# Up projections of three feed-forward layers: the order of three ScalarE operations within one unit

## The chip, the cores and the metric

One core of a Trainium2 chip runs the whole program. The time is the device time of one execution in microseconds (us). Of the kernel before there are three timed executions: 1224.78, 1225.55 and 1227.5 us, median 1225.55 us. One further execution was recorded by the hardware profiler; all rows below come from it.

## The reference

The input is 256 tokens of 1024 channels in float32. One layer of a first kind is followed by two layers of a second kind. Each layer projects the tokens, mixes them in three branches (attention, a recurrence or a pooling, a gated convolution or a second attention), adds the result to the stream, normalizes, and ends with a feed-forward part. The feed-forward part is what matters here:

```
u  = causal_conv3(h @ w_up)        # 1024 -> 2 * 2816 channels, 3 taps over the tokens
a, b = split(u, 2)
x  = x + act(a) * b @ w_down       # act: gelu in the first layer, silu in the two others
```

## The kernel before, in words

Channels stand on the 128 partitions and the 256 tokens on the free axis. All weights stream from HBM once, in 400 *units* of 128 output channels by up to 1024 input channels (512 KB, or 448 KB for seven blocks). To keep float32 accuracy TensorE works with split operands: a weight tile `raw` becomes a high part `whi` (a rounded copy, ScalarE, line 735) and a low part `wlo = raw - whi` (VectorE, line 1393), and each 128x128 block takes three matmuls: `whi` with the high activations (line 1067), `whi` with the low ones (1068), `wlo` with the high ones (1069). A whole unit is 24 matmuls.

`raw`, `whi` and `wlo` are rings of three tiles. Unit n waits on TensorE for `wlo` of unit n (`split_lo`). ScalarE may write `whi` of unit n+3 when unit n is done on TensorE (`unit_done`) and the load has landed (`arrived`). SyncE issues the load of unit n+3 when VectorE has written `wlo` of unit n. The result banks in PSUM are also a ring of three.

Each engine has its own instruction stream, written out in a fixed order, and works through it in order. There is no planner in this part. The up projection of a layer has 44 units: even ones give a tile of `a` (the gate), odd ones the matching tile of `b`. The first six and the last eight units are written out, those between run in a hardware loop of six. I call the units of one up projection 0 to 43, and those of the down projection behind it 44, 45, 46 and so on. The three stages are `up1` (first layer), `up20` and `up21`.

The work on one up unit, in the order of the engines' programs:

- ScalarE (`ffn`, lines 991 to 1020): the high part of the unit two ahead; then it waits for the unit; the eviction (lines 1007, 1009: it reads the bank, scales by the last tap and writes `ugate` or `uval`). After an odd unit it applies the activation to `ugate` (line 1014), after an even unit it waits for GpSimd's product of the pair before and copies it to `fhi` (`high`, line 995).
- VectorE (`up`, lines 1731 to 1743): the low part of the unit two ahead (line 1393), then the two other taps, which read the bank (lines 1738, 1741). The second one frees the bank.
- GpSimd (`ffn`, lines 621 to 641): for each pair the product `fprod = ugate * uval` (line 636), which waits for both taps and for the activation; and then the low part `flo` of the pair before (line 625). For the last pair the low part stands alone behind the loop.

The first activation of each up projection is preceded by a load of ScalarE's function table. The down projection (24 units of 8, 7 and 7 blocks) needs all 22 tiles of `fhi` and `flo`: its third unit, number 46, waits for `flo` of the last tile (line 1332). Between an up projection and what precedes it stands a normalization. Units 0 and 1 are computed interleaved, block by block, as the normalized tiles come in; in `up20` and `up21` GpSimd is meanwhile still writing the residual stream (line 702).

Of the kernel before, what the change touches and what calls it, by code (L numbers as in the profile page):

```python
# [16 lines left out]
UPT = 2 * FT  # L17
# [34 lines left out]
def unit_table():  # L52

    units, start = [], {}

    def phase(name, array, tiles, parts):
        start[name] = len(units)
        for t in range(tiles):
            at = 0
            for n in parts:  # L60
                units.append((array, t, at, n))
                at += n

    start["win1"] = 0
    units += [("w_win1", t, 0, 8) for t in PLAN1]
    phase("merge1", "w_merge1", KT, (8, 8))
    phase("wout1", "w_out1", KT, (8,))
    phase("up1", "w_up1", UPT, (8,))
    phase("down1", "w_down1", KT, DOWN_PARTS)
    for l in range(LAYERS2):  # L70
        start[f"win2{l}"] = len(units)
        units += [(f"w_win2{l}" if kind == "in" else f"w_merge2{l}", t, 0, 8) for kind, t in PLAN2]
        phase(f"wout2{l}", f"w_out2{l}", KT, (8,))
        phase(f"up2{l}", f"w_up2{l}", UPT, (8,))
        phase(f"down2{l}", f"w_down2{l}", KT, DOWN_PARTS)
    return units, start


UNITS, START = unit_table()
# [120 lines left out]
def build(nc, args, out):  # L200
# [3 lines left out]
    with ctx:  # L204
# [137 lines left out]
        def wait(eng, s, base, it=0, per=0):  # L342

            if isinstance(it, int):
                if base + it * per > 0:
                    eng.wait_ge(s, base + it * per)
            else:
                eng.wait_ge(s, it * per + base)

        def repeat(eng, name, count, per, body, peel_first=False):  # L350

            rounds = count // per
            lo, hi = (1 if peel_first else 0), rounds - 1
            n0 = START[name]
            for i in range(lo * per):
                body(n0 + i, i, 0)
            if hi > lo:
                with eng.Fori(lo, hi) as it:  # L360
                    for i in range(per):
                        body(n0 + i, i, it)
            for i in range(hi * per, count):
                body(n0 + i, i, 0)
# [34 lines left out]
        def tile(ten, t, it=0, per=0):  # L399

            return ten[:, t:t + 1, :] if isinstance(it, int) else ten[:, bass.ds(it * per + t, 1), :]

        def tap(cols, width, k, i, it):

            a = COLS[cols] + width * i + k
            return vec[:, a:a + 1] if isinstance(it, int) else vec[:, bass.ds(it * (6 * width) + a, 1)]
# [35 lines left out]
        def bank_of(r):  # L442
            return unit_bank[r % 3]
# [283 lines left out]
        def _(act):  # L727
            def hi_part(n, it=0, per=0):
                if n >= len(UNITS):
                    return  # L730
                blocks = UNITS[n][3]

                wait(act, arrived[n % RING], 16 * (n // RING + 1), it, 16 * per // RING)
                wait(act, unit_done, n - RING + 1, it, per)
                act.activation(whi[:, n % RING, 0:blocks * P], raw[:, n % RING, 0:blocks * P], ACT.Copy).then_inc(split_hi, 1)  # L735
# [255 lines left out]
            def ffn(f, name, cols, silu):  # L991
                def high(t, it=0):

                    wait(act, product, FT * f + t + 1, it, 3)
                    act.activation(tile(fhi, t, it, 3), tile(fprod, t % 3), ACT.Copy).then_inc(f_hi, 1)  # L995

                def body(n, i, it):
                    if i or not isinstance(it, int):
                        hi_part(n + 2, it, 6)
                    p, r = FT * f + i // 2, (i // 2) % 3  # L1000
                    wait(act, unit_done, n + 1, it, 6)

                    wait(act, product, p - 2, it, 3)

                    ps, dst = bank_of(RESULT[name] + i)[:, 0:S], (ugate, uval)[i % 2][:, r, :]
                    if silu:
                        act.activation(dst, ps, ACT.Copy, scale=tap(cols, 3, 2, i, it)).then_inc(conv_start, 1)
                    else:
                        act.activation(dst, ps, ACT.Identity, scale=tap(cols, 4, 2, i, it), bias=tap(cols, 4, 3, i, it)) \
                            .then_inc(conv_start, 1)  # L1010
                    if i % 2:

                        wait(act, conv_done, KT + 2 * p + 1, it, 6)
                        act.activation(ugate[:, r, :], ugate[:, r, :], ACT.Silu if silu else ACT.Gelu_apprx_tanh).then_inc(gelued, 1)
                    elif i or not isinstance(it, int):
                        high(i // 2 - 1, it)

                repeat(act, name, UPT, 6, body, peel_first=True)
                hi_part(START[name] + UPT + 2)
                high(FT - 1)  # L1020

            wout(START["wout1"], "ffn")
# [1 line left out]
            hi_part(START["up1"] + 2)  # L1024
            norm_hi("ffn", dev)
            ffn(0, "up1", "ffn_1", False)
            down("down1", "final")
            norm_root("final", RMS_EPS)
# [3 lines left out]
            for l in range(LAYERS2):  # L1032
                first = START[f"win2{l}"]
                waiting = None
                for p, (kind, t) in enumerate(PLAN2):
                    n = first + p
                    if kind == "in":
                        act.wait_ge(unit_done, n + 1)
                        ps = bank_of(RESULT[f"win2{l}"] + p)[:, 0:S]
                        dst = pads[:, 0, t - 6, 16:16 + S] if t in (6, 7) else u2[:, t, :]  # L1040
                        if t < 14:
                            act.activation(dst, ps, ACT.Copy).then_inc(copied, 1)
                        else:
                            act.activation(dst, ps, ACT.Tanh, scale=0.5).then_inc(copied, 1)
                    steps(n, first + MIX2)
                    if waiting is not None:
                        merged_hi(KT * (1 + l), waiting)
                    waiting = t if kind == "merge" else None
                merged_hi(KT * (1 + l), KT - 1)
                wout(START[f"wout2{l}"], f"ln1{l}", 1)  # L1050
                norm_root(f"ln1{l}", LN_EPS)
                hi_part(START[f"up2{l}"] + 2)
                norm_shift(f"ln1{l}", False)
                ffn(1 + l, f"up2{l}", f"ffn_2{l}", True)
                down(f"down2{l}", f"ln2{l}")
                norm_root(f"ln2{l}", LN_EPS)
                if l < LAYERS2 - 1:
                    hi_part(START[f"win2{l + 1}"] + 2)
                norm_shift(f"ln2{l}", l == LAYERS2 - 1)
# [860 lines left out]
```

## Time and profile before

| what | value |
|---|---|
| median of three executions | 1225.55 us |
| profiled execution, its own time | 1226.56 us |
| span from the first to the last instruction in it | 1224.7 us |
| mean granted TensorE clock | 0.993 |
| TensorE matmul busy | 1206.6 us (99%) |
| TensorE weight load busy | 1183.0 us (97%) |
| VectorE busy | 846.1 us (69%) |
| ScalarE busy | 707.7 us (58%) |
| GpSimd busy | 406.6 us (33%) |
| mean of DMA over the span | 174 GB/s |

The busy time of TensorE counts matmuls that overlap in its pipeline: one is recorded with some 0.28 us although the next starts much sooner. So a lost moment is best read from the starts of two neighbouring matmuls, not from the busy share. Idle time that the profile shows in brackets is counted from the modelled end of the matmul before.

### The profile page before, as it was taken

The numbers are of one execution on the slowest core, as the hardware profiler recorded it, in microseconds if no ns is written. First come the engines' busy times: TensorE is split into PE (matmuls) and PEld (weight loads), VectorE is DVE, ScalarE is ACT, GpSimd is POOL, SyncE is SP. The second block draws the span as 40 slices with busy tenths as digits, with TensorE's granted clock in tenths as the row PEclk, the third lists the DMA queues.
The fourth block names the chain that finished last, engine by engine and source line by source line (L and its number), as shares of the span: only waits on it lengthen the run. The fifth ranks groups of instructions, "written<-read, shape, count | busy, mean of one in ns | idle before, by whom it ended". The sixth has DMA issues, their size and how long they took to land. (4 is left out here: it accounts for less than half of the span.)

```text
span 1224.7 us, 27264 instructions
## 1 busy us (share of the span) xinstructions
PE 1206.6 (99%) x10242; PEld 1183.0 (97%) x10242; DVE 846.1 (69%) x1458; ACT 707.7 (58%) x1228; POOL 406.6 (33%) x376
## 2 busy tenths in 40 slices
PE   8999999999999999999999999999999999999997
PEld 8999999999999999999999999999999999999997
DVE  6868666677777755766677777656766677777655
ACT  5667676445766654566455666644566555666642
POOL 3007304123334302200338343314500348344313
PEclk9999999999999999999999999999999999999998
DMA  7555455664666665555653666664555654666662
GB/s 254 183 168 156 134 153 166 197 182 154 194 187 201 183 191 162 164 164 155 190 185 116 183 190 187 195 190 147 171 157 156 190 187 121 178 199 186 196 189 85
DMA packets 60288, 212.70 MB, mean 174 GB/s; under 512 B 6688, under 2 KB 7968, under 8 KB 60064
## 3 DMA queue, kind: packets, MB, share of 16 engines
q1 hardware_dynamic: 60192, 211.39, 56.6%
q8 instruction: 65, 1.06, 0.4%
q14 instruction: 31, 0.25, 0.1%
HBM read 210.31 MB, written 1.05 MB: 173 GB/s over the span
## 5 line engine op out<-in xcount | busy, mean ns | idle before, releaser
L1393 DVE TENSOR_TENSOR wlo<-raw,whi 128x1024 fp32r<-128x1024 f32 (+1 forms) x400 | 488.5, 1222 | 289.4 <-ACT whi L735 287.5
L1067 PE MATMUL bank<-shifted,whi 128*128 128x256 f32 x2296 | 638.9, 278 | 1.5 <-POOL shifted L669 1.1
L1068 PE MATMUL bank<-shifted,whi 128*128 128x256 f32 x2296 | 636.3, 277 | 0.0
L1069 PE MATMUL bank<-shifted,wlo 128*128 128x256 f32 x2296 | 636.0, 277 | 0.0
L735 ACT ACTIVATE whi<-raw 128x1024 fp32r<-128x1024 f32 (+1 forms) x400 | 415.6, 1040 | 148.0 <-PE bank L1069 134.4
L1067 PEld LDWEIGHTS bank<-shifted,whi 128*128 128x128 f32 x2296 | 431.7, 188 | 3.1 <-POOL shifted L669 1.3
L1069 PEld LDWEIGHTS bank<-shifted,wlo 128*128 128x128 f32 x2296 | 431.7, 188 | 0.0
L1068 PEld LDWEIGHTS bank<-shifted,whi 128*128 128x128 f32 x2296 | 431.1, 188 | 0.0
L636 POOL TENSOR_TENSOR fprod<-ugate,uval 128x256 f32<-128x256 f32 x66 | 99.4, 1506 | 210.1 <-DVE uval L1741 204.5
L1067 PE MATMUL bank<-fhi,whi 128*128 128x256 f32 x528 | 146.8, 278 | 0.0
L1069 PE MATMUL bank<-fhi,wlo 128*128 128x256 f32 x528 | 146.5, 277 | 0.0
L1068 PE MATMUL bank<-flo,whi 128*128 128x256 f32 x528 | 146.5, 277 | 0.0
L650 POOL TENSOR_TENSOR u<-u,tmp 128x256 f32<-128x256 f32 x48 | 53.7, 1119 | 234.1 <-DVE tmp L1696 232.0
L1067 PE MATMUL bank<-aligned,whi 128*128 128x256 f32 x334 | 105.2, 315 | 4.2 <-DVE wlo L1393 2.2
L1069 PEld LDWEIGHTS bank<-fhi,wlo 128*128 128x128 f32 x528 | 99.7, 189 | 0.0
L1067 PEld LDWEIGHTS bank<-fhi,whi 128*128 128x128 f32 x528 | 99.1, 188 | 0.1
L1068 PEld LDWEIGHTS bank<-flo,whi 128*128 128x128 f32 x528 | 99.1, 188 | 0.0
L1069 PE MATMUL bank<-aligned,wlo 128*128 128x256 f32 x334 | 93.3, 279 | 0.0
L1068 PE MATMUL bank<-aligned,whi 128*128 128x256 f32 x334 | 92.4, 277 | 0.0
L995 ACT ACTIVATE fhi<-fprod 128x256 f32 (+1 forms) x66 | 27.6, 418 | 100.4 <-POOL fprod L636 100.4
L1067 PEld LDWEIGHTS bank<-aligned,whi 128*128 128x128 f32 x334 | 62.8, 188 | 14.4 <-issue 9.0
L1068 PEld LDWEIGHTS bank<-aligned,whi 128*128 128x128 f32 x334 | 62.9, 188 | 0.7
(212 smaller groups left out, 1283.3 us busy)
## 6 DMA issues: line engine op xcount, KB each, us to landing
raw<-in_w_win SPq DMA_DIRECT2D x140, 512.0 KB, 3.6
raw<-in_w_up SPq DMA_DIRECT2D x132, 512.0 KB, 3.6
raw<-in_w_down SPq DMA_DIRECT2D x48, 448.0 KB, 3.8
raw<-in_w_merge SPq DMA_DIRECT2D x32, 512.0 KB, 4.1
raw<-in_w_out SPq DMA_DIRECT2D x24, 512.0 KB, 3.8
raw<-in_w_down SPq DMA_DIRECT2D x24, 512.0 KB, 3.6
x<-in_x SPq DMA_DIRECT2D x4, 256.0 KB, 3.9
rgw<-in_rg_w SPq DMA_DIRECT2D x1, 1024.0 KB, 10.2
```

Source lines behind the costliest of these rows:

```text
L636: pool.tensor_tensor(tile(fprod, t % 3), tile(ugate, t % 3), tile(uval, t % 3), ALU.mult).then_inc(product, 1)
L650: ins = pool.tensor_tensor(m, m, branch_part(base, t, branch), ALU.add)
L735: act.activation(whi[:, n % RING, 0:blocks * P], raw[:, n % RING, 0:blocks * P], ACT.Copy).then_inc(split_hi, 1)
L995: act.activation(tile(fhi, t, it, 3), tile(fprod, t % 3), ACT.Copy).then_inc(f_hi, 1)
L1067: pe.matmul(ps, whi[:, slot, w], hi, start=first, stop=False)
L1068: pe.matmul(ps, whi[:, slot, w], lo, start=False, stop=False)
L1069: return pe.matmul(ps, wlo[:, slot, w], hi, start=False, stop=last)
L1393: dve.tensor_tensor(wlo[:, n % RING, w], raw[:, n % RING, w], whi[:, n % RING, w].bitcast(f32), ALU.subtract) \
```

## The change

The high part of a unit is now issued by the body of the unit three before it, behind the eviction and in front of the activation (odd units) or of the wait for the product and its copy (even units). Before, it was issued at the head of the body of the unit two before it. Between two evictions the order was therefore eviction, activation or copy, high part; now it is eviction, high part, activation or copy. The set of instructions, their tiles and their semaphores stay the same; the high part that stood behind the loop is now issued by the last body.

```diff
                 def body(n, i, it):
-                    if i or not isinstance(it, int):
-                        hi_part(n + 2, it, 6)
                     p, r = FT * f + i // 2, (i // 2) % 3
                     wait(act, unit_done, n + 1, it, 6)
...
                         act.activation(dst, ps, ACT.Identity, scale=tap(cols, 4, 2, i, it), bias=tap(cols, 4, 3, i, it)) \
                             .then_inc(conv_start, 1)
+                    hi_part(n + 3, it, 6)
                     if i % 2:
 
                         wait(act, conv_done, KT + 2 * p + 1, it, 6)
...
                 repeat(act, name, UPT, 6, body, peel_first=True)
-                hi_part(START[name] + UPT + 2)
                 high(FT - 1)
```

## Rows read from the trace of the kernel before

**Rows 1.** Windows: stretch, its length, busy us and instructions by engine, PEclk, DMA share, GB/s.
```profile
311.00:418.00 107.00, 107.00 (x940) 107.00 (x939) 81.26 (x119) 70.68 (x118) 44.68 (x40) 1.00 0.64 194
...
849.60:853.00 3.40, 3.31 (x14) 2.92 (x13) 2.95 (x8) 2.18 (x4) 3.40 (x5) 0.50 0.00 0
```
**Rows 2.** Waits of TensorE: who waited for whom, us in total, times, longest us.
```profile
PE bank L1067 <- DVE wlo L1393: 2.2, 2, 1.1
```
**Rows 3.** Timeline, TensorE early in up20: start us, us, engine, line, tiles.
```profile
670.93 0.28 PE L1069 MATMUL bank<-shifted,wlo 128*128 128x256 f32 x1
...
671.54 0.28 PE L1068 MATMUL bank<-aligned,whi 128*128 128x256 f32 x1
...
674.13 0.28 PE L1069 MATMUL bank<-shifted,wlo 128*128 128x256 f32 x1
...
675.70 0.28 PE L1068 MATMUL bank<-aligned,whi 128*128 128x256 f32 x1
```
**Rows 4.** Timeline, VectorE's low parts of units 4 and 5 in up20.
```profile
669.93 1.33 DVE L1393 TENSOR_TENSOR wlo<-raw,whi 128x1024 fp32r<-128x1024 f32 x1 [0.90 <-ACT whi L735]
...
674.19 1.23 DVE L1393 TENSOR_TENSOR wlo<-raw,whi 128x1024 fp32r<-128x1024 f32 x1 [2.02 <-ACT whi L735]
```
**Rows 5.** Timeline, ScalarE early in up20, from the eviction of unit 1.
```profile
666.75 0.47 ACT L1007 ACTIVATE uval<-bank,vec 128x256 f32<-128x256 f32 x1
667.23 1.28 ACT L1014 ACT_TABLE_LOAD   x1
668.53 0.42 ACT L1014 ACTIVATE ugate<-ugate 128x256 f32<-128x256 f32 x1
668.85 1.05 ACT L735 ACTIVATE whi<-raw 128x1024 fp32r<-128x1024 f32 x1
669.80 0.45 ACT L1007 ACTIVATE ugate<-bank,vec 128x256 f32<-128x256 f32 x1
672.79 0.42 ACT L995 ACTIVATE fhi<-fprod 128x256 fp32r<-128x256 f32 x1 [2.54 <-POOL fprod L636]
673.12 1.04 ACT L735 ACTIVATE whi<-raw 128x1024 fp32r<-128x1024 f32 x1
```
**Rows 6.** Timeline, TensorE at the third unit of the down projection behind up20.
```profile
788.39 0.28 PE L1069 MATMUL bank<-fhi,wlo 128*128 128x256 f32 x1
...
789.18 0.28 PE L1068 MATMUL bank<-aligned,whi 128*128 128x256 f32 x1
```
**Rows 7.** Timeline, end of up20: the last eviction on ScalarE.
```profile
783.73 0.45 ACT L1007 ACTIVATE uval<-bank,vec 128x256 f32<-128x256 f32 x1
```
**Rows 8.** Timeline, end of up20: VectorE.
```profile
783.85 1.09 DVE L1393 TENSOR_TENSOR wlo<-raw,whi 128x896 fp32r<-128x896 f32 x1 [1.01 <-ACT whi L735]
...
785.38 0.48 DVE L1741 SCALAR_TENSOR_TENSOR uval<-bank,vec,uval 128x254 f32<-128x254 f32 x1
```
**Rows 9.** Timeline, end of up20: GpSimd.
```profile
785.93 1.52 POOL L636 TENSOR_TENSOR fprod<-ugate,uval 128x256 f32<-128x256 f32 x1 [2.71 <-DVE uval L1741]
787.41 1.43 POOL L625 TENSOR_TENSOR flo<-fprod,fhi 128x256 fp32r<-128x256 f32 x2
```
**Rows 10.** Timeline, TensorE at unit 4 of up1 and at unit 46 behind it.
```profile
308.49 0.28 PE L1069 MATMUL bank<-shifted,wlo 128*128 128x256 f32 x1
...
309.06 0.28 PE L1068 MATMUL bank<-aligned,whi 128*128 128x256 f32 x1
...
423.54 0.28 PE L1069 MATMUL bank<-fhi,wlo 128*128 128x256 f32 x1
...
424.09 0.28 PE L1068 MATMUL bank<-aligned,whi 128*128 128x256 f32 x1
```
**Rows 11.** Timeline, TensorE at unit 5 of up21.
```profile
1040.98 0.28 PE L1069 MATMUL bank<-shifted,wlo 128*128 128x256 f32 x1
...
1042.61 0.28 PE L1068 MATMUL bank<-aligned,whi 128*128 128x256 f32 x1
```
**Rows 12.** DMA issues: tiles, queue, count, KB each, median us from issue to landing.
```profile
raw<-in_w_up SPq DMA_DIRECT2D x132, 512.0 KB, 3.6
```

## The prediction

> **What bounds the kernel now.** I read the windows first. In the quiet middle of up1 TensorE starts 940 matmuls in 107.00 us at a granted clock of 1.00, its level of 2.4 GHz: one every 0.114 us, without a hole [rows 1]. A unit of 24 takes 2.73 us, and no reordering on ScalarE shortens that. What such a change can give back is the sum of the places where TensorE waited for something behind ScalarE's queue. So I read TensorE's waits next: two long ones, 2.2 us in all, are for `wlo` at the head of a unit [rows 2]. Then I went along the timeline of TensorE and looked in the three up projections for two matmul starts further apart than 0.114 us. Three places stand out in up20; I measure each from the last matmul of one unit to the second of the next, less two steps (0.23 us), which also catches the slow restart of the first matmul:
>
> - unit 4: 670.93 to 671.54, lost 0.38 us [rows 3];
> - unit 5: 674.13 to 675.70, lost 1.34 us [rows 3];
> - unit 46, the third of the down projection: 788.39 to 789.18, lost 0.56 us [rows 6].
>
> up21 has the same three: its unit 5 loses 1.40 us [rows 11], and the two others repeat up20's within 0.04 us (0.38 and 0.60). up1 has two small ones, 0.34 us at unit 4 and 0.32 us at unit 46 [rows 10]. The sum over the three layers is 0.66 + 2.28 + 2.38 = 5.3 us, 0.43% of the time. That is the ceiling for the direct gain.
>
> **Unit 4 and unit 5: why they wait.** The low part of unit 4 ends at 671.26, that of unit 5 at 675.42, each just ahead of the matmul that starts late; both times VectorE had been idle until the high part was there [rows 4]. On ScalarE the first activation brings a table load of 1.28 us. Behind the eviction of unit 1 at 666.75 come table load, activation, and only at 668.85 the high part of unit 4; then the eviction of unit 2, a wait of 2.54 us for the first product of GpSimd, its copy at 672.79, and only at 673.12 the high part of unit 5 [rows 5]. Both high parts needed nothing of what stood ahead of them.
>
> **The same stretch in the new order**, with durations of these rows and the pipelining that they show (the next activation starts about 0.1 us before the recorded end of the one before):
>
> - ScalarE: high part of unit 4 from 667.2 to 668.25, table load to 669.55, activation to 669.95, eviction of unit 2 from 669.9 to 670.35 (0.1 later than now), high part of unit 5 from 670.3 to 671.35, copy of the product still at 672.8 (GpSimd sets it), eviction of unit 3 from 673.1, high part of unit 6 to 674.6.
> - Load of unit 5: it goes out when the low part of unit 2 is written, so before TensorE starts unit 2, two units ahead of unit 4, at about 671.04 - 5.46 = 665.6; with a median landing of 3.6 us [rows 12] it is there by 669.2, ahead of 670.3.
> - VectorE keeps its order (low part of unit n+2, taps of unit n, 0.5 us each). The low part of unit 4 now follows the taps of unit 1 and ends at about 670.3; TensorE wants it at 671.04. The low part of unit 5 ends at 672.6; wanted at 673.8. The low part of unit 6 follows the taps of unit 3 and ends at 675.9; wanted at 676.5.
>
> Unit 5 then has 1.2 us to spare. What is late next is unit 6, with 0.6 us; its term hangs on GpSimd's first product. I count both holes as gone: 0.38 + 1.34 in up20, 0.38 + 1.40 in up21, and 0.34 in up1, where the same table load stands: 3.84 us. Bounds: 2.5 us, if half an us reappears at unit 6 in the two late layers and up1 keeps its hole, and 3.84 us, since the holes can't give more.
>
> **Inside the loops** the edit costs and gives nothing: there is no hole now. The cover is the ring of three: after an eviction a bank is wanted two units (5.5 us) later, and the activation and the copy are pushed back by one high part, 1.05 us. The copy at even units waited for the product anyway, so the high part fills that idle time. A high part asked for earlier must find its load landed. Its issue hangs on the low part three units before, which moves forward as well: the landing comes some 1.5 us ahead of the request at the median of 3.6 us, and a late one holds ScalarE, not TensorE.
>
> **Unit 46** waits for `flo` of the last tile. The chain before it: last eviction at 783.73, just behind the end of unit 43 on TensorE (the next unit starts 44 steps before 788.39, at 783.4), so it can't move; VectorE is at that moment busy with the low part of unit 45 until 784.94, and only then the two taps, to 785.86 [rows 7, 8]; product 785.93 to 787.45, two low parts to 788.84 [rows 9]. In the new order the high part of unit 45 stands ahead of the copy, its low part is over before the last eviction, and the taps end at 785.25. But the last activation now stands behind the high part of unit 46: 784.2 to 785.15, activation to 785.5. So the product starts at 785.5 instead of 785.93. The activation takes the place of the taps as what ends last: 0.45 us gained of 0.6. I take 0.47 us in up20 and 0.5 in up21. In up1 evictions are 0.57 us long and the low part is started no later than here, so I take half its hole, 0.15. Sum 1.1 us. Bounds: from -0.6 us (three times 0.2, if the activation ends later than the taps do now) to 1.5 us, the whole holes.
>
> A rule of the skill bears on the product. The row shows it at 1.52 us here, and it overlaps the low part of unit 46 on VectorE [rows 9]. The Trainium skill, "SBUF — State Buffer", section "SBUF: two separate sides", says that GpSimd and a two-input VectorE operation take a shared port pair as an exclusive lock, so that the second one waits for the whole first. By that rule the product ends 0.6 us behind the low part of unit 46 whenever it starts inside it; the end would then move by how much that low part moves, again about 0.45 us, so the sum stays as it is.
>
> **Sum.** 3.84 + 1.1 = 4.9 us. The profiled execution would go from 1226.56 us to 1221.7 (span 1219.8). It is 1.0 us above the median of the runs, so for the median 1225.55 - 4.9 = 1220.7 us.
>
> **The rivals.**
>
> *The hole moves to unit 6.* For it: GpSimd writes the residual stream until just before the first product, and ScalarE waits for it (2.54 us, [rows 5]) ahead of the eviction of unit 3, on which the low part of unit 6 now hangs. Against it: 0.6 us of room. Price: with a product 1.3 us later 0.7 us come back in each of two layers. Gain 3.5 us, 1222.1 us.
>
> *The table load first empties ScalarE's pipeline.* The load would then wait for the end of the high part ahead of it and hold what follows by as much again, one high part (1.05 us). The eviction of unit 2 slips to 671.0, the low part of unit 5 to 673.7, and that of unit 6 to 677.0, so about 0.6 us come back per layer: gain 3.1 us, 1222.5 us. Against it: the rows show the load 0.01 us behind the end of an eviction and the activation 0.02 us behind the load [rows 5]. The Trainium skill, "ScalarE: Activation LUTs", section "What ACT_TABLE_LOAD costs", gives 1283 ns for the load, which the trace confirms with 1.28 us, and about 1380 ns of drain on top, which no row here shows. By its figure I would estimate some 0.3 us more per layer to come back.
>
> *Given back behind the up projections.* The down projections and normalizations start earlier, but their own chains (loads that land just in time, the norm's chain across four engines) do not. For it: ring and DMA work at 194 GB/s all the way [rows 1]. Against it: the loads hang on the same low parts, which come earlier. If half is lost, 1223.2 us; if all, 1225.5 us. I put the case at 1224.3.
>
> *Slower: the clock.* In a normalization TensorE idles, and the granted clock fell to 0.50 (1.2 GHz) for 3.4 us at 849.6 [rows 1], there mostly over filler matmuls. The change moves the five normalizations behind up1 in time. Where such a dip covers real products it costs half of it, 1.7 us. From three new dips (5.1 us) the gain is gone; with five it is 8.5 - 4.9 = 3.6 us slower, 1229.2 us. For it: the fall is seen in the profile; against it: it fell on filler, and nothing in the change lengthens the idle time.
>
> **How the numbers follow.** Chances: forecast 0.72, hole at unit 6 0.12, emptied pipeline 0.05, given back 0.07, clock 0.04. The predicted time is the first one's, 1220.7 us. Its bounds by the terms are 1225.55 - 5.3 = 1220.2 and 1225.55 - 1.9 = 1223.7. The three runs before lie up to 2 us above their median and 0.8 below it, so another median of few runs may lie about an us off: 1218.9 to 1223.6 us as the range, which takes in the first two rivals. A difference of 0.2% (2.45 us) is about what a measurement of this kernel can tell from no change; it lies at 1223.1. Faster: the first three cases with a little left out for scatter, 0.85; within 0.2%: 0.11, mainly gain given back; slower: 0.04.
>
> **What would show it.** Right: no start distance over 0.2 us at units 4 and 5 of up20 and up21; table load behind a high part; high part of unit 5 some 3 us ahead of the copy of the first product; the last product waiting for the activation and no longer for the taps. Wrong: a hole at unit 6 of up20, a wait of ScalarE for `raw` inside the loops that reaches TensorE, a hole of 0.3 us or more at unit 46, or a granted clock below 1.00 over real products.

## The result, and the profile after

The changed kernel takes 1218.08 us (median of four, 1217.63 to 1218.27); the kernel before 1225.82 us (median of four). The ratio is 0.9934, 95% interval 0.9923 to 0.9946: 7.7 us faster. The prediction was 1220.7 us with a range from 1218.9. The direction was right; the gain was half as large again as forecast and the time lies 0.8 us below the range. The profiled executions are further apart, 1226.56 and 1217.63 us, spans 1224.7 and 1215.8 us.

By the page of the changed kernel no engine's total moved by over 7 us, and ScalarE does the same work, 707.5 us against 707.7:

```profile
span 1215.8 us, 27264 instructions
## 1 busy us (share of the span) xinstructions
PE 1199.6 (99%) x10242; PEld 1177.9 (97%) x10242; DVE 852.5 (70%) x1458; ACT 707.5 (58%) x1228; POOL 404.3 (33%) x376
```

In the list of TensorE's waits the line for `wlo` [rows 2] is gone, and so are the waits for `flo`. The largest of what is left stand at the normalizations:

```profile
PE bank L1122 <- POOL acc L663: 3.9, 5, 2.4
PE bank L1065 <- POOL shifted L669: 1.1, 1, 1.1
```

Early in up20, ScalarE after the change (answers to [rows 5]; lines of this file behind 998 count two less, those from 1009 to 1017 one less):

```profile
663.63 0.47 ACT L1005 ACTIVATE uval<-bank,vec 128x256 f32<-128x256 f32 x1
663.99 1.06 ACT L735 ACTIVATE whi<-raw 128x1024 fp32r<-128x1024 f32 x1
665.07 1.28 ACT L1013 ACT_TABLE_LOAD   x1
666.36 0.42 ACT L1013 ACTIVATE ugate<-ugate 128x256 f32<-128x256 f32 x1
666.69 0.46 ACT L1005 ACTIVATE ugate<-bank,vec 128x256 f32<-128x256 f32 x1
667.04 1.05 ACT L735 ACTIVATE whi<-raw 128x1024 fp32r<-128x1024 f32 x1
670.17 0.42 ACT L995 ACTIVATE fhi<-fprod 128x256 fp32r<-128x256 f32 x1 [2.08 <-POOL fprod L636]
```

The high part of unit 4 now stands ahead of the table load, that of unit 5 3.1 us ahead of the copy of the product. TensorE in the same stretch, at the heads of units 4 and 5 (answers to [rows 3]):

```profile
668.12 0.28 PE L1067 MATMUL bank<-shifted,wlo 128*128 128x256 f32 x1
668.24 0.28 PE L1065 MATMUL bank<-aligned,whi 128*128 128x256 f32 x1
668.36 0.28 PE L1066 MATMUL bank<-aligned,whi 128*128 128x256 f32 x1
...
670.95 0.28 PE L1067 MATMUL bank<-shifted,wlo 128*128 128x256 f32 x1
671.07 0.28 PE L1065 MATMUL bank<-aligned,whi 128*128 128x256 f32 x1
671.18 0.28 PE L1066 MATMUL bank<-aligned,whi 128*128 128x256 f32 x1
```

The distance from the last matmul of a unit to the second of the next is 0.23 to 0.24 us at both heads, where it was 0.61 and 1.57: the holes are closed. The end of up20 after the change, ScalarE, VectorE and GpSimd (answers to [rows 7 to 9]):

```profile
778.14 0.47 ACT L1005 ACTIVATE uval<-bank,vec 128x256 f32<-128x256 f32 x1 [1.12 <-PE bank L1067]
778.51 0.95 ACT L735 ACTIVATE whi<-raw 128x896 fp32r<-128x896 f32 x1
779.36 0.41 ACT L1013 ACTIVATE ugate<-ugate 128x256 f32<-128x256 f32 x1
```
```profile
776.83 1.08 DVE L1391 TENSOR_TENSOR wlo<-raw,whi 128x896 fp32r<-128x896 f32 x1
...
779.17 0.48 DVE L1739 SCALAR_TENSOR_TENSOR uval<-bank,vec,uval 128x254 f32<-128x254 f32 x1
779.57 1.09 DVE L1391 TENSOR_TENSOR wlo<-raw,whi 128x896 fp32r<-128x896 f32 x1
```
```profile
779.89 1.36 POOL L636 TENSOR_TENSOR fprod<-ugate,uval 128x256 f32<-128x256 f32 x1 [3.25 <-DVE uval L1739]
781.21 1.44 POOL L625 TENSOR_TENSOR flo<-fprod,fhi 128x256 fp32r<-128x256 f32 x2
```

From the last eviction to the start of the last product it is 1.75 us; before it was 2.20, so 0.45 us less, as forecast. The product starts behind the activation (ends at 779.77) and no longer behind the taps (779.65), also as forecast; the row names VectorE as the releaser, but the activation's semaphore comes 0.11 us behind that of the taps. To the end of `flo` it is 4.51 us against 5.11.

Where the rest came from shows only when the times of the semaphore events are laid out by stage. For each stage this table has the time from the end of the last unit of the stage before to the end of its own last unit, before and after, the difference, and how many units were *slow*: the median distance of their matmul starts is over 0.1155 us.

```
stage        before    after    diff   slow units before / after
win1         226.20   225.76   -0.44   19 / 19
up1          126.77   126.25   -0.51    2 /  0
down1         62.72    60.56   -2.15   18 /  0
up20         132.19   129.83   -2.36    7 /  4
down20        61.80    61.00   -0.79    1 /  0
up21         131.60   129.66   -1.95    3 /  2
down21        61.84    61.00   -0.84    1 /  0
all others   421.62   421.75   +0.13   13 / 14
```

The biggest surprise is down1: 2.15 us in a stage whose code did not change. TensorE's step there, in windows of 37 us, first the kernel before, then the changed one:

```profile
438.00:475.00 37.00, 37.00 (x316) 37.00 (x315) 18.30 (x20) 16.37 (x20) 5.83 (x4) 1.00 0.66 196
```
```profile
438.00:475.00 37.00, 37.00 (x329) 37.00 (x329) 19.31 (x21) 16.67 (x22) 5.83 (x4) 1.00 0.70 203
```

316 matmuls against 329, at a granted clock of 1.00 in both: a mean step of 0.117 us against 0.1125, with no wait shown anywhere. By single starts within a unit TensorE has two steps, 0.118 and 0.1133 us; every unit of down1 from number 50 on runs at the longer one before, and none after. Where it begins, VectorE's low part of unit 50 and TensorE at the head of that unit, in the kernel before:

```profile
433.16 1.23 DVE L1393 TENSOR_TENSOR wlo<-raw,whi 128x1024 fp32r<-128x1024 f32 x1 [2.07 <-ACT whi L735]
```
```profile
434.45 0.28 PE L1069 MATMUL bank<-fhi,wlo 128*128 128x256 f32 x1
434.57 0.34 PE L1067 MATMUL bank<-fhi,whi 128*128 128x256 f32 x1
434.75 0.28 PE L1068 MATMUL bank<-flo,whi 128*128 128x256 f32 x1
434.87 0.28 PE L1069 MATMUL bank<-fhi,wlo 128*128 128x256 f32 x1
```

The low part is written at 434.39, the last matmul of unit 49 starts at 434.45; the second start of unit 50 comes 0.18 us behind its first, and from there on all distances are 0.118 us.

### The profile page after: what moved, and what is told of

It reads as the page before. It is cut to its first block, busy times and chain, and to the rows that moved or that the text cites. A ratio compares the mean times of both kernels' runs of the same rounds, so it can differ in the third digit from the quotient of the medians.

```text
span 1215.8 us, 27264 instructions
## 1 busy us (share of the span) xinstructions
PE 1199.6 (99%) x10242; PEld 1177.9 (97%) x10242; DVE 852.5 (70%) x1458; ACT 707.5 (58%) x1228; POOL 404.3 (33%) x376
## 4 chain that ended last, share of the span: by engine, by line
PE 89%; issue 4%; DVE 3%; POOL 3%; ACT 1%; DMA 0%; POOLq 0%; DVEq 0%; ACTq 0%
PE bank L1065 28%; PE bank L1067 27%; PE bank L1066 27%; POOL acc L663 2%; PE bank L1206 1%; PE bank L1237 1%; PE bank L1122 1%; PE bank L1081 1%; DVE wlo L1391 1%; PE bank L1217 1%; POOL acc L659 1%; PE bank L1261 1%; ACT whi L735 0%; POOL u L650 0%; PE bank L1193 0%
## 5 line engine op out<-in xcount | busy, mean ns | idle before, releaser
L1067 PEld LDWEIGHTS bank<-aligned,wlo 128*128 128x128 f32 x334 | 62.6, 187 | 0.0
```

The lines of the kernel that those rows point to most:

```text
L1067: return pe.matmul(ps, wlo[:, slot, w], hi, start=False, stop=last)
```

## The experiments

A margin below is the time from the writing of a unit's low part to the moment when TensorE wants it, at the last matmul start of the unit before. I call a short irregular step at the head of a unit a stumble. Each kernel is compared with the kernel before on its own chip: 1225.59 us in the first group, 1226.1 in the second, 1225.88 in the last. Microseconds of gain are differences of medians; the ratio with its interval, given beside them, puts those of the edits to the kernel before lower, by 0.3 to 0.9 us, and by 1.3 us in b_odd.

**b_sines**, the kernel before with one edit in down1, where unit 50 had a margin of 0.06 us:

```diff
-                    if name == "down1" and i == 3 and isinstance(it, int):
+                    if name == "down1" and i == 4 and isinstance(it, int):
                         step_prepare_sines()
                         load_sqrt()
```

> The kernel before, with one edit in the down projection of the first layer: the two sines and the table loads around them stand one body later, so that the high part of unit 50 goes ahead of them. Theory A (near miss): in the kernel before, the low part of unit 50 is written only 0.06 us before TensorE wants it, TensorE falls there into a step of 0.118 us per matmul instead of 0.113 and keeps it for the 18 units to the end of the stage, 1.8 us. With the high part earlier by over 2 us the step stays at 0.113: 1.8 us faster than before, near 1224.0 us. Theory B: the longer step belongs to the stage itself (its loop, its tiles) or is an accident of one execution: no change, within 0.5 us of before.

Measured: 1224.67 us (11 runs), ratio 0.9995, 95% interval 0.9986 to 1.0004. In the profile unit 50 has a margin of 2.21 us, no unit of down1 is slow, and down1 takes 60.74 us instead of 62.72:

```profile
438.00:475.00 37.00, 37.00 (x329) 37.00 (x328) 19.15 (x20) 16.10 (x20) 5.84 (x4) 1.00 0.70 205
```

So the trace says theory A, and the time does not decide: the medians differ by 0.9 us, half of what A gives, and the interval runs from 1.7 us faster to 0.5 us slower. Either the edit costs elsewhere, or the kernel before does not have the long step in all executions. That led to the last group.

**a_late**, the changed kernel with a tiny activation ahead of the high part of unit 50:

```diff
                         step_prepare_sines()
                         load_sqrt()
+                        act.activation(small[:, 88:89], small[:, 92:93], ACT.Copy)
```

> The changed kernel with one tiny activation (one column, about 0.2 us) added on ScalarE in the down projection of the first layer, ahead of the high part of unit 50. The low part of unit 50 there has 0.13 us to spare. Theory A: it becomes some 0.07 us late, TensorE loses 0.1 to 0.2 us at the head of that unit and then 0.1 us in each of 18 units: 1.9 us slower than the changed kernel, near 1220.0 us. Theory B: the delay itself and nothing more, 0.1 to 0.2 us: near 1218.2 us.

Measured: 1217.61 us, ratio 0.9945 (0.9931 to 0.9958). A miss for A as written. The activation cost only 0.11 us, as neighbours overlap; the margin fell to 0.04 us, unit 50 lost 0.09 us, and the short step stayed in the profiled execution. But the five times are 1217.17, 1217.61, 1217.61, 1219.04 and 1220.11, where the changed kernel's four lie within 0.64 us.

**a_sines**, the changed kernel with the edit of b_sines.

> The changed kernel with the sines one body later, as in the other run. Theory A: the margin of unit 50 was 0.13 us and just enough; nothing to win, within 0.3 us of the changed kernel (1218.1). Theory B: the same. If the changed kernel still lost in some executions to the longer step, its spread would shrink and its median fall.

Measured: 1217.57 us (1217.45 to 1217.93), margin 2.29 us, down1 60.56 us as in the changed kernel. Nothing to win there, as both theories said. It is not a faster version that I could tell from the changed kernel (0.9938 against 0.9934, with intervals 0.0025 wide).

**b_loop, b_start, b_end**: the kernel before with the high part moved only in some bodies. The edit is the same in all, with `early` as `not isinstance(it, int)` (loops), `isinstance(it, int) and i < 6` (start) and `isinstance(it, int) and i >= 36` (end):

```diff
-                    if i or not isinstance(it, int):
-                        hi_part(n + 2, it, 6)
...
+                    if early:
+                        hi_part(n + 3, it, 6)
                     if i % 2:
...
+                    if not early:
+                        hi_part(n + 3, it, 6)
...
-                hi_part(START[name] + UPT + 2)
```

Behind the activation or the copy of one body is the same place in ScalarE's order as the head of the next, so where `early` is false the order is that of the kernel before.

> The new order only in the hardware loops (units 6 to 35 of the three up projections); the first six and last eight units in the old one. Theory A: the low parts of the odd units, which in the kernel before run down to margins of 0.1 us and below, get 2 us; the three stumbles in the loops (units 21 and 33 of up20, unit 31 of up21) go: 0.33 + 0.33 + 0.2 = 0.9 us faster, near 1224.9 us; the holes at units 4, 5 and 46 stay; down1 keeps its longer step unless unit 50's margin moves by chance. Theory B, that of my prediction (nothing to gain inside the loops): no change.

Measured: 1222.59 us, ratio 0.9981 (0.9972 to 0.9990): 3 us faster, not 0.9 and not nothing. In the profile up20 lost 1.01 us and up21 0.24, mostly the stumbles; and down20 and down21 lost 0.79 and 0.84, since the margin at the heads of units 46 and 47 depends on what the loop hands over. Down1 lost the long step, but its unit 46 starts 0.67 us later.

> The new order only in the first six units of each up projection, the old one in the loops and in the last eight. By the direct count of the starts the holes at units 4 and 5 go, 3.8 us; what the near misses in the loops do is open: the margins at the loop's start are larger, so that they may never run down to zero, which would give another 0.9 us. Near 1221.5 us, 1220.9 at best. Rival: the stall moves to unit 6, only 2.5 us gained.

Measured: 1221.03 us, ratio 0.9964 (0.9950 to 0.9977), 5.1 us faster. up1, up20 and up21 lost 0.51, 2.27 and 2.21 us: the holes, and of the stumbles those of up21. With a better start the margins of up21's loop stay at 0.11 us and more. Those of up20 still ran down to -0.04 us by unit 33: its units 21, 27 and 33 took 2.83, 2.88 and 2.91 us where 2.74 is due, though none turned slow. Unit 6 did not become a hole (margin 0.11 us, 0.02 us lost). Down1 took 63.70 us: 0.8 us longer at unit 46, and the long step for that unit and all that followed. The reason for the 0.8 us, at the end of up1 of b_start, VectorE and GpSimd, and TensorE at unit 46 (VectorE's lines count two more here than in the kernel before):

```profile
419.91 1.61 DVE L1395 TENSOR_TENSOR wlo<-raw,whi 128x896 fp32r<-128x896 f32 x1
422.04 1.23 DVE L1395 TENSOR_TENSOR wlo<-raw,whi 128x1024 fp32r<-128x1024 f32 x1 [0.51 <-ACT whi L735]
```
```profile
419.84 0.74 POOL L636 TENSOR_TENSOR fprod<-ugate,uval 128x256 f32<-128x256 f32 x1 [2.71 <-DVE uval L1743]
420.54 3.31 POOL L625 TENSOR_TENSOR flo<-fprod,fhi 128x256 fp32r<-128x256 f32 x2
```
```profile
423.99 0.35 PE L1069 MATMUL bank<-aligned,whi 128*128 128x256 f32 x1 [0.77 <-POOL flo L625]
```

The product starts 0.07 us ahead of the low part and takes 0.74 us, and the low part takes 1.61 instead of 1.09. In the changed kernel and in the one before the low part was first and the product took 1.36 and 1.52 us [rows 9]. The first `flo` operation then runs beside the rest of this low part and takes 1.59 us, the second beside the next low part, which starts 0.05 us ahead of it, and takes 1.76: 3.31 us for the two instead of 1.43. That agrees with the Trainium skill, "SBUF — State Buffer", section "Who interferes with whom": the order of issue decides which of the two is held.

> The new order only in the last eight units of each up projection. The holes at unit 46 and the restarts at unit 47 go: 0.3 + 0.8 + 0.8 = 1.9 us. In the first layer TensorE then comes to unit 50 0.3 us earlier and ScalarE about as much: margin as in the changed kernel or as in the one before; if the former, the longer step goes as well and it is 3.7 us in all. Between 1222.1 and 1223.9 us.

Measured: 1222.91 us, ratio 0.9978 (0.9968 to 0.9987), 3.2 us faster, inside what I gave. Down1 60.56, down20 61.00, down21 61.00 us, to the hundredth what they are in the changed kernel. So for the down stages the last eight units are enough. The three parts give 3.0, 5.1 and 3.2 us, more than the 7.7 of the whole, since two of them can each remove the same stumbles, the same holes at unit 46 (b_loop and b_end both have down20 and down21 at 61.00 us) and the same long step.

**b_odd and b_even**: the same edit with `early = i % 2 == 1` (ahead of the activation) and `early = i % 2 == 0` (ahead of the copy).

> The high part ahead of the activation at odd units only; at even units it stays behind the copy of the product. The hole at unit 4 goes (1.1 us over three layers), that at unit 5 stays, since its high part still stands behind the first product. Even units at the end gain little. If the activation is the culprit of half: 1.1 to 2.0 us faster, near 1224 us.

Measured: 1224.99 us, ratio 1.0002 (0.9993 to 1.0012): no gain that can be told by the ratio, though the median is 1.1 us lower; a miss. In up20 the hole at unit 4 is gone, and units 2 to 5 together still take 12.71 us against 12.84: unit 5 starts when its low part is there, and that has not moved. ScalarE shows why: the high part of unit 5 starts behind the copy, and the copy waits for GpSimd, whose time the edit doesn't move.

```profile
668.22 0.46 ACT L1005 ACTIVATE ugate<-bank,vec 128x256 f32<-128x256 f32 x1
671.16 0.42 ACT L995 ACTIVATE fhi<-fprod 128x256 fp32r<-128x256 f32 x1 [2.49 <-POOL fprod L636]
671.49 1.04 ACT L735 ACTIVATE whi<-raw 128x1024 fp32r<-128x1024 f32 x1
```

> The high part ahead of the wait for the product and its copy at even units only; at odd units it stays behind the activation. The hole at unit 5 goes (2.8 us), that at unit 4 stays; unit 46 gains (the low part of unit 45 is early, and the last activation stands ahead of the high part of unit 46, so the last product starts earlier than in the changed kernel): all of 1.9 us. The odd units' margins, which run down in the loops, hang on this high part: 0.9 us more. Some 5 us faster, near 1220.5 us; the odd part alone then does little.

Measured: 1220.58 us, ratio 0.9962 (0.9950 to 0.9975), 5.5 us faster, as forecast. up20 lost 2.43 and up21 1.74 us with no slow unit in up20, and down20 and down21 are at 61.00 us. The even units carry the change.

**again1, again2, again3**: the kernel before, unchanged, for more profiles; and **a_late2**, the changed kernel with an activation of 256 columns in place of the tiny one:

```diff
+                        act.activation(probT[:, 0, 0:S], const[:, 0:S], ACT.Copy)
```

> The kernel before once more, unchanged, for another profile. What is open is whether the longer step of down1 (18 units at 0.118 us per matmul, 1.8 us in all) is the same in every execution. Theory A (a near miss with a coin toss): the margin at unit 50 is the same 0.06 us each time, and the step stays short in some executions and turns long in others; an execution with the short step takes down1 in some 60.9 us, one with the long step 62.7. Theory B (fixed by the program): down1 takes 62.7 us in each.

> The same as again1, a second profile. Theory A: the two may differ by 1.8 us in down1. Theory B: they don't.

> The same as again1, a third profile. Theory A and B as there.

Measured, with the first profile of the kernel before:

```
             before   again1   again2   again3
time        1226.56  1225.72  1224.42  1224.87
margin u.50    0.06     0.05     0.04     0.04
unit 50        2.89     2.89     2.82     2.82
down1         62.72    62.58    60.93    60.93
slow units       18       18        0        0
```

The same program, the same margin, two outcomes 1.7 us apart: theory A. (b_odd, whose unit 50 has a margin of 0.05 us, is a third profile without the long step in down1.) TensorE in again2, in the same window as above:

```profile
438.00:475.00 37.00, 37.00 (x329) 37.00 (x328) 19.07 (x20) 16.62 (x21) 5.83 (x4) 1.00 0.68 207
```

The stumbles of the loops come and go as well: in again2 unit 21 of up20 takes 2.77 us, in the first profile 2.98 us with a slow unit behind it. So does the hole at unit 4 of up20: in again1 and again3 unit 4 takes 2.78 us, and units 2 and 3 are 0.2 us longer together instead.

> The changed kernel with an activation of 256 columns (0.3 us net) ahead of the high part of unit 50 in down1: its low part is some 0.2 us late in every execution. Theory A: each execution pays the hole and its restart, 0.2 to 0.4 us, and a share of them 1.8 us more for the longer step; the times fall into two groups, near 1218.0 and near 1220 us. Theory B (the delay alone counts): one group near 1218.0 us with the narrow spread of the changed kernel.

Measured: 1217.86, 1218.76, 1219.34, 1219.43 and 1220.94 us, median 1219.34. Margin -0.18 us in the profile, unit 50 takes 3.12 instead of 2.72 us, all 18 units are slow, down1 62.62 us instead of 60.56:

```profile
438.00:475.00 37.00, 37.00 (x316) 37.00 (x316) 19.16 (x20) 15.43 (x20) 5.81 (x4) 1.00 0.66 199
```

So 0.3 us of ScalarE time at this place cost 2.06 us in that execution. The times spread over 3 us; two clean groups they are not. The ratio, 0.9946 (0.9932 to 0.9961), does not part it from the changed kernel, but four of the five times lie above all nine of the changed kernel and a_sines. Theory B, a narrow group near 1218.0 us, falls.

**Margins over all profiles.** The 14 profiles of these kernels hold 2303 units of the up and down projections, from the sixth of each on, that follow a unit at the short step. Of the 2178 with a margin over 0.115 us none took 0.02 us more than is due and none turned slow (by the mean of its last eight distances). Of the 125 with less, 28 turned slow. So in these stages the longer step set in only where a low part came late or less than 0.12 us early; in which of those cases it does is not explained.

## Why the prediction was wrong

The forecast was 4.9 us of gain and the medians show 7.7. Of the 2.8 us between them the term for unit 46 has some 0.9, the loops, put at nothing, 0.9, and down1, which stood in no term, 0.9. With them the ceiling of 5.3 us falls as well: it counted only holes of over 0.3 us. The range, too, left little room there: 1.3 us below the bound of 1220.2 us.

**Unit 4 and unit 5.** Right, in mechanism and size. I had 3.84 us for the three layers. From the durations of units 2 to 6 in up20 and the same in up1 and up21 it is 3.8 us: 0.38, 1.57 and 1.81. up20 stayed below its term since units 2 and 3 there run 0.09 and 0.20 us longer after (low part of unit 3 late by 0.09 us). That is scatter and no cost of the change: a_late2 and a_sines have these units at 2.74 us, and again1 and again3 have them longer in the kernel before. So the close hit is in part luck of the two profiles. b_odd shows that the two holes are one chain, and that the hole at unit 4 alone was worth nothing where another stood behind it; my sum added them, which holds only because both went.

**Unit 46.** The chain came as written, but the term was mis-sized: I took 1.1 us of gain at the three ends, the traces give 0.33 + 0.79 + 0.84 = 1.96. Two things were left out. The head of unit 47 had lost 0.2 us in each late layer, which I had not looked at (2.94 and 2.95 us where 2.72 is due; 2.85 to 2.87 us in again1 to again3). And the product got shorter, 1.36 instead of 1.52 us, since VectorE's low part, which holds it, had moved forward by 0.6 us and not by the 0.45 that I set. The bound of 1.5 us was too low for the first reason.

**"Inside the loops the edit costs and gives nothing: there is no hole now."** This is the step that failed. I looked for idle time and took a row of up1 [rows 1] for all three loops. In up20 and up21 the low part of every second unit arrived mostly 0.1 to 0.4 us before it was wanted, but 0.05 and 0.04 us too late at units 21 and 33 of up20 and only 0.08 us early at unit 31 of up21: these are the three stumbles, 0.86 us in the profile. After the change the margin in the loops is some 2 us. b_loop measures the step by itself: 3 us by the medians, where I had nothing. Some 1.2 us of that show inside up20 and up21, the rest in the down stages, to which the loops hand on their margins.

**Down1** stood in no term. The stumble at unit 50 at a margin of 0.06 us put TensorE on the longer step for 18 units: 1.83 us of the profile's 8.9. In half of the four profiles of the kernel before it did so, thus, as an estimate from four draws, some 0.9 us of the mean. That also accounts for the profile's larger difference (8.9 against 7.7 of the medians), with 0.44 us in win1, a stage that the change doesn't touch and that varies by as much between profiles of one kernel.

The sum with what was measured: 3.8 + 2.0 + 0.9 + 1.8 + 0.4 = 8.9 us for the profiled pair, against 3.8 + 1.1 forecast.

**The rivals.** No hole opened at unit 6 of up20 (margin 0.54 us, 0.6 forecast). In up21 the margin there is only 0.11 us, and units 6 and 7 run at the longer step, 0.17 us in all; a_sines and a_late2 show the same. The room that the forecast gave this rival was not there in up21. No emptying of the pipeline: the table load starts 0.02 us behind the end of the high part, and the activation 0.01 us behind the load; the drain that the Trainium skill adds in "ScalarE: Activation LUTs", "What ACT_TABLE_LOAD costs", would not fit in between. Nothing was given back: the stages not named agree to 0.13 us in all. The clock: there are again two dips in the normalizations ahead of up20 and win21, at 652.5 and 843.6 us, mostly over filler (matmuls of `ones` whose result nobody reads), mean clock 0.994 against 0.993.

```profile
843.60:847.00 3.40, 3.35 (x13) 3.18 (x14) 2.95 (x6) 1.93 (x4) 3.40 (x5) 0.50 0.00 0
```

**Open.** What in TensorE holds the longer step, and what ends it. In up20 it ended after one or two units, in down1 not before the stage's end. No run here tells whether the loads, the loop or the tiles decide this. It also stands in the same 19 units of win1 in all 14 profiles, at margins of 0.4 to 4.4 us, so a late low part is not its only way in. In unit 11 of win1, for one, it follows four matmuls of another product (`rgw`) 0.215 us apart and a restart of 0.307 us. Whether any uneven start can bring it in was not tried.

## What to carry to other kernels

A producer that arrives just in time is not free. List for each consumer step the margin between ready and wanted, not only the waits: here margins of 0.06 us and less cost 0.07 us or more on the spot and, by chance, 2 us behind it, while the margin of 0.09 us at unit 47 of the changed kernel cost nothing in any profile. In an in-order queue, put what feeds the bottleneck ahead of everything that waits for a third engine; the even units, where the wait for GpSimd stood in front, gave 5.5 of the 7.7 us by the medians (4.7 by the ratio). A single profile of a kernel with such margins is one draw: profile it two or three times before its time is split up.

## What the runs showed of the hardware

TensorE runs this stream of weight loads and matmuls at 0.1133 us per matmul or at 0.118, at the same granted clock of 1.00, 4% apart. A low part that comes late or less than 0.12 us early can switch it to the longer step (28 of 125 such units, none of 2178 others), and it may stay there for 18 units with all later low parts over 1 us early. The busy rows show nothing of it: TensorE is 100% busy in either; only the count of matmuls in a window does.

Two GpSimd operations that take 1.43 us together took 3.31 us when each ran beside a two-input VectorE operation that had begun before it, and the VectorE operation 1.61 instead of 1.09 us when the GpSimd one was 0.07 us ahead.
